# Another distribution of expert dots over a hybrid decoder step's stages, and whole dots that read x from PSUM

## The chip, the cores and the metric

One core of a Trainium2 chip runs the whole program. The metric is the device time of one execution in microseconds; lower is better. PE is the matrix engine, VectorE (DVE) and ScalarE (ACT) compute on tiles, GpSimd (POOL) here issues the indirect DMAs, SyncE (SP) the plain ones.

## What is computed

One layer of a decoder in float32, for a prompt of 1024 tokens and for eight sequences of four new tokens (32 rows, "the sample") that attend to 1024 cached tokens each. Cut to what matters here:

```python
xn = rms_norm(x, attn_norm_w); q_lat, c_kv, k_pe, rq, rk, rv, rg = split(xn @ w_in)
h = x + concat([attention(q, k, v), silu(rg) * group_norm(retention(rq, rk, rv))]) @ w_o
# the PEER feed-forward, on xb = rms_norm(h, ffn_norm_w)
q = (xb @ w_peer_q).reshape(n, 8, 2, 128)
s1, s2 = q[:, :, 0] @ sub_keys1.T, q[:, :, 1] @ sub_keys2.T     # 8 heads, 128 keys each
v1, i1 = top_k(s1, 16); v2, i2 = top_k(s2, 16)
vs, ic = top_k(v1[..., :, None] + v2[..., None, :], 16)          # 16 experts of 16384 per head
act = gelu(einsum('nd,nhkd->nhk', xb, peer_u[experts]))          # the dots
y = h + einsum('nhk,nhkd->nd', softmax(vs) * act, peer_v[experts])
```

Each of the 1024 tokens picks 8 x 16 = 128 experts, and each expert is one row of 4 KB in `peer_u` and one in `peer_v`.

## The kernel before

The prompt is worked in eight tiles of 128 tokens; the sample is a ninth tile, numbered 8, of 32 tokens, whose attention is threaded into tiles 1, 2 and 3. Tokens lie on the 128 partitions. A **slot** is the work on the k-th expert of every token of a tile: 128 slots a tile, and for the sample 32 (its 32 tokens are spread over 128 partitions). A slot has two halves. First the **u row**: POOL gathers 128 rows of `peer_u` into one of 8 buffers (`u_ring`, `u_rows`, L799), and VectorE multiplies it with x and sums, the **dot** (`dot`, L1776), in two instructions of 512 columns, each followed by an accumulator read, with a partial sum each in `dots_2` and `dots`. For each group of 32 slots VectorE adds the partial sums, ACT applies gelu (L1346), VectorE the gates and a transpose, and ACT writes the coefficients into the matrix Z (`make_Z`). Then the **v row**: POOL gathers 128 rows of `peer_v` into one of 9 buffers (`v_rows`, L816), and PE adds them, weighted by Z, into two PSUM banks (`v_row`, L856), 33 slots behind the dots (`V_LAG`). POOL issues v and u rows in turn; a u row waits for the dot that frees its buffer, a v row for PE.

All else of the tile, its **front**, is written out by hand on each engine in the same order of stages: PROJECT (ten weight pieces; in tiles 2, 4 and 6, the hosts, also those of the next tile, their guest), QKV (heads, norms, retention), ATTEND (ten steps, one head each with a shift between scores, probability transposes and the product with v), in tile 1 the sample's mixer, in tiles 2 and 3 a batch of cached pages of four sequences, OUT (output projection, norm), PEER (nine steps; step s holds PE's queries of head s and VectorE's selections of head s - 1). Heads 6 and 7 of a tile are selected during the next tile's PROJECT.

What sets the order is a **pace**. Between the pieces of the front every engine calls `slots()` at the same numbered places, the **sites**. Tables of numbers (`FRONTS`, `PEER`, `LAST`, L543 to L557) say by how many slots the work advances at each site; `sites()` (L559) sums them into bounds, and at a site VectorE computes the dots up to its bound, PE the v rows up to the bound less 33, ACT what falls due of gelu, Z and results. The slots run one tile behind: the front of tile t carries slots of tile t - 1 until step `TURN_OVER` = 4 of its PEER stage, and the first of its own behind. So a front of tiles 1 to 7 carries 95 slots outside PEER and 33 in it, and tile 0's PEER stage 18.

PSUM has eight banks. Banks 0 and 1 hold the v rows' sum; `bank(i)` is bank 2 + i. The keys' scores of the PEER stage lie in banks 6 and 7, the transposed probabilities of a head in bank 4 and, for tiles 4 to 7, also 5, the product with v in bank 6.

## Time and profile before

| what | value |
|---|---|
| median of 3 runs | 3480.07 us (3473.72 to 3485.91) |
| the profiled execution | 3479.65 us |
| its span in the profile | 3477.9 us |
| granted clock of PE, mean | 0.803 |
| busy: PE, DVE, ACT, POOL | 71%, 71%, 12%, 61% |
| moved by DMA | 1321.87 MB, 380 GB/s on average |
| of it the indirect queue | 1107.43 MB |

How to read it: the page gives each engine's busy time; the forty slices of the span carry, under each other, tenths of busy time, PE's clock, the DMA engines' share and GB/s. A query on windows gives the same for chosen stretches. Groups list instructions by source line and shape, with busy time, mean duration and what ended the idle time before them. Groups on DVE under L1751 and L1755 are helpers that issue most of VectorE's instructions.

### The profile page before, as it was taken

How to read it: one execution, taken by the hardware profiler on the slowest of the kernel's cores; microseconds unless marked ns; L12 is line 12 of the kernel's file. 1: busy time of each engine (PE TensorE's matmuls, PEld its weight loads, DVE VectorE, ACT ScalarE, POOL GpSimd, SP SyncE). 2: the span in 40 equal slices, each digit the busy share in tenths (PEclk: the TensorE clock that was granted, in tenths of full speed). 3: DMA queues.
4: the chain of work that ended last, by engine and by line, in shares of the span. 5: the costliest groups of instructions: out<-in, count | busy, mean ns of one | idle time of the engine just before them, and what ended most of it. 6: DMA issues, size and time to landing. Idle time of an engine off the chain costs nothing.

```text
span 3477.9 us, 37700 instructions
## 1 busy us (share of the span) xinstructions
PE 2486.0 (71%) x11828; PEld 1260.8 (36%) x11828; DVE 2468.6 (71%) x8388; ACT 432.7 (12%) x980; POOL 2135.6 (61%) x2118
## 2 busy tenths in 40 slices
PE   6768656888756687696666777697766776678567
PEld 5644124644432334362331234363331233324200
DVE  4587757768678886767578766777578766948652
ACT  1101000113101221111001110111101110000000
POOL 0136755566646665647756775647756775677876
PEclk8879677898877888898886778898887788775667
DMA  6479999999999999999999999999999999999999
GB/s 256 170 266 393 383 347 388 389 382 357 392 399 367 391 370 391 411 370 410 410 410 406 410 409 407 397 368 410 411 410 400 410 406 408 381 411 383 348 409 369
DMA packets 373386, 1321.87 MB, mean 380 GB/s; under 512 B 60962, under 2 KB 72418, under 8 KB 352962
## 3 DMA queue, kind: packets, MB, share of 16 engines
q0 software_dynamic: 304128, 1107.43, 81.2%
q1 hardware_dynamic: 69058, 212.03, 15.7%
q8 instruction: 93, 1.52, 0.2%
q14 instruction: 107, 0.88, 0.1%
HBM read 1311.41 MB, written 7.88 MB: 379 GB/s over the span
## 4 chain that ended last, share of the span: by engine, by line
PE 26%; DVE 23%; DMA 22%; POOL 17%; issue 9%; SPq 2%; ACT 1%; DVEq 0%; ACTq 0%
DMA u_ring<-up_rows,codes 10%; POOL v_ring L824 9%; POOL u_ring L811 8%; DMA v_ring<-down_rows,codesT 8%; PE ps L932 7%; DVE u_ring L1785 7%; PE ps L869 6%; DMA wbuf<-weights 4%; DVE arena L1751 3%; PE ps L922 3%; PE ps L1132 2%; PE ps L1185 2%; DVE idx L1751 1%; DVE top_c L1751 1%; DVE top_v L1751 1%
## 5 line engine op out<-in xcount | busy, mean ns | idle before, releaser
L1785 DVE CUSTOM_DVE_ANT_0 u_ring<-u_ring,xn 128x512 f32<-128x512 f32 x2112 | 1345.7, 686 | 510.7 <-DMA u_ring<-up_rows,codes 506.3
L811 POOL DMA_INDIRECT u_ring<-up_rows,codes x1056 | 1077.4, 1020 | 769.6 <-issue 291.8
L869 PE MATMUL ps<-v_ring,Z 128*32 128x512 f32 x4096 | 1082.6, 757 | 613.8 <-DMA v_ring<-down_rows,codesT 474.6
L824 POOL DMA_INDIRECT v_ring<-down_rows,codesT x1056 | 1057.0, 1001 | 559.0 <-issue 284.4
L869 PEld LDWEIGHTS ps<-v_ring,Z 128*32 128x32 f32 x4096 | 147.9, 121 | 1222.2 <-DMA v_ring<-down_rows,codesT 918.0
L1132 PEld LDWEIGHTS ps<-xT,wbuf 128*128 128x128 f32 x2176 | 312.0, 229 | 200.0 <-issue 119.1
L1132 PE MATMUL ps<-xT,wbuf 128*128 128x128 f32 (+1 forms) x2176 | 337.4, 318 | 57.1 <-DMA wbuf<-weights 57.1
L932 PE MATMUL ps<-wbuf,xT 128*128 128x256 f32 (+2 forms) x1184 | 285.4, 399 | 64.9 <-DMA wbuf<-weights 34.8
L932 PEld LDWEIGHTS ps<-wbuf,xT 128*128 128x128 f32 (+1 forms) x1184 | 226.4, 198 | 141.4 <-DMA wbuf<-weights 47.8
L1785 DVE DVE_READ_ACCUMULATOR2_ANT dots<- 128x1 f32 x2112 | 170.4, 81 | 0.0
L1751 DVE MAX8 vals<-arena 128x8 f32<-128x128 f32 (+1 forms) x288 | 68.8, 279 | 79.1 <-ACT arena L1565 78.4
L1088 PE MATMUL ps<-kT,qT 96*128 96x512 f32 (+3 forms) x192 | 103.0, 656 | 23.7 <-DVE nb L1755 19.4
L922 PE MATMUL ps<-wbuf,kT 128*128 128x256 f32 (+1 forms) x480 | 104.7, 371 | 0.0
L1527 ACT ACTIVATE arena<-arena,nb 128x128 f32<-128x128 f32 (+7 forms) x64 | 49.6, 775 | 354.7 <-DVE nb L1755 354.7
L922 PEld LDWEIGHTS ps<-wbuf,kT 128*128 128x128 f32 x480 | 88.9, 190 | 11.1
L1106 PEld LDWEIGHTS ps<-vN,arena 128*128 128x128 f32 x576 | 78.0, 211 | 8.5 <-issue 7.4
L1106 PE MATMUL ps<-vN,arena 128*128 128x64 f32 x576 | 80.1, 289 | 0.0
L1088 PEld LDWEIGHTS ps<-kT,qT 96*128 96x128 f32 x192 | 39.8, 239 | 111.2 <-issue 74.6
L1751 DVE FIND_INDEX8 idx<-vals,arena 128x8 uint32<-128x128 f32 (+1 forms) x288 | 78.1, 282 | 0.0
L1565 ACT ACTIVATE arena<-ps 128x256 f32<-128x256 f32 (+1 forms) x72 | 27.4, 380 | 371.6 <-PE ps L1142 329.7
L1557 ACT ACTIVATE arena<-ps 128x256 f32<-128x256 f32 (+1 forms) x72 | 26.3, 365 | 353.3 <-PE ps L1132 353.3
L1755 DVE TENSOR_REDUCE arena<-arena 128x8 f32<-128x512 f32 (+1 forms) x72 | 49.2, 683 | 27.4 <-ACT arena L1665 24.5
(337 smaller groups left out, 2425.2 us busy)
## 6 DMA issues: line engine op xcount, KB each, us to landing
wbuf<-weights SPq DMA_DIRECT2D x142, 1024.0 KB, 8.2
u_ring<-up_rows,codes POOLq DMA_INDIRECT x1056, 12.3
v_ring<-down_rows,codesT POOLq DMA_INDIRECT x1056, 12.2
u_ring<-weights SPq DMA_DIRECT2D x8, 1024.0 KB, 13.5
v_ring<-weights SPq DMA_DIRECT2D x8, 1024.0 KB, 13.8
wbuf<-weights SPq DMA_DIRECT2D x9, 768.0 KB, 7.7
resid<-x_prompt SPq DMA_DIRECT2D x8, 512.0 KB
table<-decay_in SPq DMA_DIRECT2D x8, 512.0 KB
```

Of the source, the lines that this page charges most:

```text
L811: pool.indirect_dma_start(out=u_ring[:, i % U_RING, :], out_offset=None, in_=up_rows, in_offset=bass.IndirectOffsetOnAxis(ap=codes[:, t % ...
L824: pool.indirect_dma_start(out=v_ring[:, v % V_RING, :], out_offset=None, in_=down_rows, in_offset=bass.IndirectOffsetOnAxis(ap=codesT[:, t ...
L869: mm = pe.matmul(acc[q:q + 32, half, :], (Zs if t == TILES else Z)[:, at:at + GS], v_ring[:, v % V_RING, half * 512:(half + 1) * 512], sta ...
L922: mm = pe.matmul(ps[:, 2 + S_BANK[w // 2], (w % 2) * PIECE:(w % 2) * PIECE + cols], xT_of(t + 1)[:, c], weights_of(t, w)[:, c, 0:cols], st ...
L932: mm = pe.matmul(out, xT[:, c, 0:n], weights_of(t, w)[:, c, 0:cols], start=(c == 0), stop=(c == DC - 1))
L1088: mm = pe.matmul(ps[:, 2 + c // 512, 0:e - c], qT[0:QK, s, :], kT[0:QK, s, c:e], start=True, stop=True)
L1106: mm = pe.matmul(ps[:, 6, h * 64:(h + 1) * 64], probT[:, h % 2, j * P:(j + 1) * P], vN[:, j, h * 64:(h + 1) * 64], start=(j == 0), stop=(j ...
L1132: mm = pe.matmul(ps[:, 4 + s % 2, j * P:j * P + n], weights_of(t, w)[:, c, j * P:(j + 1) * P], xT[:, c, 0:n], start=(c == 0), stop=(c == D ...
L1185: pe.matmul(ps[0:n, 6 + m % 2, :], lhs, uk, start=True, stop=True).then_inc(kn_ps, 1)
L1527: own.raises(act.activation(scores[:, s % 2, 0:w], scores[:, s % 2, 0:w], ACT.Exp, bias=nb[:, s:s + 1], scale=SCALE, accum_out=sums[:, s:s ...
L1751: own.done(instruction_of(*args, **kwargs))
L1785: ins = dve.tensor_tensor_reduce(u, u, xn[:, t % 2, of], 1.0, 0.0, ALU.mult, ALU.add, into)
```

## The change

The tables get other numbers. Slots of the front by stage, summed from the tables (before, after):

| tile | PROJECT | QKV | ATTEND | mixer or batch | OUT | PEER |
|---|---|---|---|---|---|---|
| 0 | 0, 0 | 0, 0 | 0, 0 | | 0, 0 | 18, 32 |
| 1 | 23, 26 | 12, 12 | 12, 10 | 37, 21 | 11, 8 | 33, 33 |
| 2 | 22, 33 | 12, 9 | 12, 10 | 37, 32 | 11, 11 | 33, 33 |
| 3 | 19, 25 | 12, 12 | 14, 11 | 40, 36 | 11, 11 | 33, 33 |
| 4 and 6 | 23, 34 | 15, 16 | 40, 27 | | 17, 18 | 33, 33 |
| 5 and 7 | 18, 26 | 18, 20 | 43, 31 | | 16, 18 | 33, 33 |
| sample | | | | | 32, 32 | 52, 52 |

The last site carries 58 slots before and 62 after. `TURN_OVER` is 5: a tile's own slots begin one step later in PEER, but in tile 0, which has a table of its own, two steps earlier. Tile 0 selects all eight heads in its own PEER stage.

In ATTEND from its third site, OUT and PEER (tiles 1 to 3: from the end of the mixer or batch) ACT copies x into banks 6 and 7, once for the slots of the tile before and once for the tile's own, and a dot is then one instruction of 1024 columns whose x comes from PSUM. These are 512 of the 1024 prompt slots; the first three own slots of a tile stay halves. The sample's 32 dots read x from the banks in which PE spreads it, and ACT's two copies of it go. To free banks 6 and 7, key scores move to banks 2 and 3, the product with v to bank 5, and the transposed probabilities of tiles 4 to 7 share bank 4: PE turns four blocks, then multiplies, then waits for VectorE's copy of the four and turns the rest, which ACT copies. PE waits for the last copied key scores before the next tile's first transposes, and for the last whole dot before piece 4 of PROJECT. Only halved dots are still summed in pairs.

```diff
+        x_now = ps[:, 6:8, :]
+        x_spread = ps[:, 2:4, :]
...
-        PROJECT = [3, 3, 4, 4, 3, 3]
-        QKV = [3, 2, 3, 3, 2, 2]
-        ATTEND = [4] * H + [5, 5]
+        PROJECT = [4, 4, 4, 5, 4, 4]
+        QKV = [2] * 6
+        ATTEND = [4] * H + [4, 4]
...
-            FRONTS[t] = [3, 3, 4, 4, 4, 5] + QKV + [4] * H + [4, 4] + [4, 3, 4, 2, 2, 2]
+            FRONTS[t] = [4, 5, 5, 5, 8, 7] + [2, 3, 3, 2, 4, 2] + [3] * 7 + [2, 2, 2] + [5, 3, 3, 2, 3, 2]
...
+        FIRST_PEER = [[0, 0], [0, 0], [0, 2], [3, 3], [3, 3], [3, 3], [2, 3], [2, 3], [1, 1]]
-        TURN_OVER = 4
+        TURN_OVER = 5
...
             def project_all(t, n, slots):
+                if t:
+                    pe.wait_ge(keys_copied, H * t)
                 turn(t, 0, mix, n)
...
                     if t and w == 4:
-                        pe.wait_ge(keys_copied, H * t)
+                        pe.wait_ge(dot_done, X_RANGES[t - 1][1])
...
-                    for j in range(t + 1):
-                        mm = pe.transpose(ps[:, 4 + j // 4, (j % 4) * P:(j % 4 + 1) * P],
-                                          scores[:, (s - 1) % 2, j * P:(j + 1) * P], ident[:])
+                    for j in range(min(t + 1, 4)):
+                        mm = pe.transpose(ps[:, 4, j * P:(j + 1) * P], scores[:, (s - 1) % 2, j * P:(j + 1) * P], ident[:])
                     mm.then_inc(probT_ps, 1)
...
+                if 1 <= s <= H and t >= 4:
+                    pe.wait_ge(probT_a, H * (t - 4) + s)
+                    for j in range(4, t + 1):
+                        mm = pe.transpose(ps[:, 4, (j - 4) * P:(j - 3) * P], scores[:, (s - 1) % 2, j * P:(j + 1) * P], ident[:])
+                    mm.then_inc(probT2_ps, 1)
...
+            def load_x(t, of_own):
+
+                if of_own:
+                    act.wait_ge(dot_done, t * SLOTS)
+                    act.wait_ge(wide_ready, wide_no(t, 2))
...
+                own.raises(act.activation(x_now, src, ACT.Copy), x_loaded, 2 * t - 1 + of_own)
...
+                load = x_load_of(i)
+                if load:
+                    dve.wait_ge(x_loaded, load)
...
+                if load or t == TILES:
+                    u = u_ring[:, i % U_RING, :].rearrange("p (a b) -> p a b", a=2)
+                    ins = dve.tensor_tensor_reduce(u, u, x_spread if t == TILES else x_now, 1.0, 0.0, ALU.mult, ALU.add, dots[:, k:k + 1])
+                else:
...
             HEADS_HERE = 6
+            WHOLE = (0, TILES - 1, TILES)
...
-                here = HEADS_HERE if t + 1 < TILES else H
+                here = H if t in WHOLE else HEADS_HERE
```

How the built program moves. VectorE in tile 0's PEER stage, behind the codes of head 1 (`codes`, their transpose `codesT`); `MAX vals` opens a head's selection and `ISA u_ring,dots` is half a dot. Before:

```order
L2057 SCALAR_TENSOR_TENSOR codes<-e 128x16
L1755 STREAM_TRANSPOSE codesT<-codes 128x32
L1751 MAX vals<-arena 128x8 x2
L1751 MAX_INDEX idx<-vals,arena 128x8 x2
L1751 MATCH_REPLACE arena<-vals,arena 128x128 x2
```

and of the change:

```order
L2143 SCALAR_TENSOR_TENSOR codes<-e 128x16
L1828 STREAM_TRANSPOSE codesT<-codes 128x32
L1865 ISA u_ring,dots<-u_ring,xn 128x512
L1865 ISA dots 128x1
L1865 ISA u_ring,dots<-u_ring,xn 128x512
```

The first dots now stand right behind head 1, where head 2 came before.

PE in ATTEND of tile 4, one step: scores (`kT,qT`), transposes of the head before (`ident,arena`), product with v (`vN,arena`), v rows (`v_ring,Z`, two instructions a row). Before:

```order
L1088 MATMUL ps<-kT,qT 128x512
L1088 MATMUL ps<-kT,qT 128x128
L1097 MATMUL ps<-ident,arena 128x128 x5
L1106 MATMUL ps<-vN,arena 128x64 x5
L869 MATMUL ps<-v_ring,Z 32x512 x8
```

and of the change:

```order
L1134 MATMUL ps<-kT,qT 128x512
L1134 MATMUL ps<-kT,qT 128x128
L1143 MATMUL ps<-ident,arena 128x128 x4
L1151 MATMUL ps<-vN,arena 128x64 x5
L1157 MATMUL ps<-ident,arena 128x128
L912 MATMUL ps<-v_ring,Z 32x512 x6
```

The fifth transpose moves behind the product with v and stands behind a wait; three v rows follow instead of four.

VectorE in OUT of tile 1, behind the mixer, of the change alone: whole dots (`u_ring,ps`) around the two additions to `resid`, where pairs of halves stood before.

```order
L1860 ISA u_ring,dots<-u_ring,ps 128x1024
L1860 ISA dots 128x1
L1824 TENSOR_TENSOR resid<-resid,ps 128x512
L1860 ISA u_ring,dots<-u_ring,ps 128x1024
L1860 ISA dots 128x1
```

Here a dot has one instruction and one accumulator read.

## Rows read from the trace of the kernel before

**Rows 1.** The page: GB/s in the forty slices of the span, and the sum.
```profile
GB/s 256 170 266 393 383 347 388 389 382 357 392 399 367 391 370 391 411 370 410 410 410 406 410 409 407 397 368 410 411 410 400 410 406 408 381 411 383 348 409 369
DMA packets 373386, 1321.87 MB, mean 380 GB/s; under 512 B 60962, under 2 KB 72418, under 8 KB 352962
```

**Rows 2.** Windows: length, busy PE, PEld, DVE, ACT, POOL, then PEclk, DMA share, GB/s.
```profile
139.00:207.90 68.90, 23.57 (x177) 22.36 (x175) 66.08 (x272) 6.93 (x18) 24.78 (x25) 0.68 0.66 225
207.90:257.30 49.40, 46.27 (x211) 31.41 (x211) 36.90 (x144) 4.49 (x12) 18.78 (x20) 0.96 0.93 337
353.00:476.40 123.40, 73.40 (x292) 16.51 (x292) 95.44 (x270) 5.97 (x20) 87.62 (x79) 0.65 0.94 359
634.10:764.40 130.30, 112.48 (x579) 78.89 (x579) 87.08 (x297) 19.09 (x40) 71.03 (x72) 0.92 0.99 382
796.10:909.50 113.40, 94.05 (x507) 46.17 (x511) 95.02 (x258) 35.99 (x74) 70.41 (x73) 0.82 0.95 357
1195.90:1316.40 120.50, 96.47 (x525) 45.94 (x526) 99.28 (x272) 35.74 (x73) 77.25 (x79) 0.84 0.95 355
1461.20:1598.30 137.10, 119.08 (x599) 78.88 (x599) 92.16 (x311) 19.10 (x40) 77.15 (x78) 0.91 0.99 385
2242.70:2378.00 135.30, 116.17 (x599) 76.97 (x601) 92.68 (x311) 18.97 (x40) 77.38 (x79) 0.94 0.99 383
2747.40:2860.40 113.00, 82.39 (x401) 36.42 (x400) 79.73 (x233) 19.71 (x34) 82.11 (x83) 0.88 1.03 407
3114.70:3280.50 165.80, 122.63 (x482) 60.03 (x482) 125.90 (x489) 8.47 (x27) 127.25 (x97) 0.57 0.97 373
```

**Rows 3.** Timeline of POOL, then VectorE, sample PEER stage: start us, us, instruction.
```profile
3184.77 4.54 POOL L811 DMA_INDIRECT u_ring<-up_rows,codes  x1 [0.30 <-issue]
...
3184.76 0.67 DVE L1785 CUSTOM_DVE_ANT_0 u_ring<-u_ring,xn 128x512 f32<-128x512 f32 x1
3185.37 0.68 DVE L1785 CUSTOM_DVE_ANT_0 u_ring<-u_ring,xn 128x512 f32<-128x512 f32 x1
...
3188.44 0.07 DVE L1785 DVE_READ_ACCUMULATOR2_ANT dots<- 128x1 f32 x1
```

**Rows 4.** Timeline of POOL, then VectorE, attention of tile 7.
```profile
2795.68 0.94 POOL L824 DMA_INDIRECT v_ring<-down_rows,codesT  x1 [0.30 <-issue]
2796.92 0.94 POOL L811 DMA_INDIRECT u_ring<-up_rows,codes  x1 [0.31 <-issue]
...
2795.70 0.70 DVE L1785 CUSTOM_DVE_ANT_0 u_ring<-u_ring,xn 128x512 f32<-128x512 f32 x1
2796.33 1.21 DVE L1988 CUSTOM_DVE_ANT_0 arena<-ps,table 128x1024 f32<-128x1024 f32 x1
2797.48 0.08 DVE L1988 DVE_READ_ACCUMULATOR2_ANT mx<- 128x1 f32 x1
```

**Rows 5.** Groups of VectorE, then PE, 2747 to 2860 us (attention of tile 7).
```profile
L1988 DVE CUSTOM_DVE_ANT_0 arena<-ps,table 128x1024 f32<-128x1024 f32 x8 | 9.8, 1221 | 4.5 <-PE ps L1088 3.9 <-issue 0.6
L1755 DVE COPY arena<-ps 128x512 f32<-128x512 f32 x8 | 5.5, 690 | 0.9
...
L869 PE MATMUL ps<-v_ring,Z 128*32 128x512 f32 x172 | 39.7, 683 | 27.6 <-DMA v_ring<-down_rows,codesT 23.4 <-ACT Z L1366 4.2
L1106 PE MATMUL ps<-vN,arena 128*128 128x64 f32 x128 | 15.3, 273 | 0.0
```

**Rows 6.** Timeline of VectorE: first head, second head, first dot of tile 0.
```profile
130.97 0.49 DVE L1751 MAX8 vals<-arena 128x8 f32<-128x128 f32 x2 [8.11 <-ACT arena L1565]
...
139.02 0.49 DVE L1751 MAX8 vals<-arena 128x8 f32<-128x128 f32 x2
...
160.91 0.69 DVE L1785 CUSTOM_DVE_ANT_0 u_ring<-u_ring,xn 128x512 f32<-128x512 f32 x1
```

**Rows 7.** Groups of POOL, 3114.7 to 3280.5 us (sample PEER stage).
```profile
L811 POOL DMA_INDIRECT u_ring<-up_rows,codes x49 | 69.1, 1411 | 24.2 <-issue 14.0 <-DVE dots L1785 10.2
L824 POOL DMA_INDIRECT v_ring<-down_rows,codesT x48 | 59.1, 1231 | 14.6 <-issue 12.8 <-PE ps L869 1.8
```

More of the change, by code:

```diff
@@ L563, in sites @@
                 at = (t - 1) * SLOTS + sum(sum(two) for two in PEER[TURN_OVER:])
-                if t < TILES:
+                if t == 0:
+                    at, sizes, before, after = 0, [0] * len(FRONTS[0]), sum(FIRST_PEER, []), []
+                elif t == 1:
+                    at = sum(sum(two) for two in FIRST_PEER)
+                if t == 0:
+                    pass
+                elif t < TILES:
                     sizes = FRONTS[t]
@@ L573, in sites, with x_ranges, x_load_of, halved @@
             return bounds
+        def x_ranges():
+            ends, at = [], 0
+            bounds = sites()
+            peer_sites = 2 * (H + 1)
+            for t in range(TILES):
+                first = at + len(PROJECT + QKV) + (2 if t not in (S_TILE,) + B_TILES else len(FRONTS[t]) - len(PROJECT + QKV) - len(OUT) + 1)
+                at += len(FRONTS[t]) + peer_sites
+                ends.append((bounds[first - 1], bounds[at - 1]))
+            return ends
+        X_RANGES = x_ranges()
+        def x_load_of(i):
+            for t in range(1, TILES):
+                begin, end = X_RANGES[t]
+                if begin <= i < t * SLOTS:
+                    return 2 * t - 1
+                if t * SLOTS + 3 <= i < (end if t < TILES - 1 else TILES * SLOTS):
+                    return 2 * t
+            return 0
+        def halved(group):
+            split = [group < GROUPS * TILES and not x_load_of(group * GS + j) for j in range(GS)]
+            begins = [j for j in range(GS) if split[j] and not (j and split[j - 1])]
+            ends = [j + 1 for j in range(GS) if split[j] and not (j + 1 < GS and split[j + 1])]
+            return list(zip(begins, ends))
+        def sums_upto(group):
+            return sum(len(halved(g)) > 0 for g in range(group + 1))
         class Pace:
@@ L1346, in gelu @@
             def gelu(t, g):
-                act.wait_ge(dots_summed, group_no(t, g) + 1)
+                act.wait_ge(dot_done, t * SLOTS + (g + 1) * GS)
+                if halved(group_no(t, g)):
+                    act.wait_ge(dots_summed, sums_upto(group_no(t, g)))
                 at = slice(g * GS, (g + 1) * GS)
@@ L1375, in put_y @@
                 own.raises(act.activation(ybuf, acc.rearrange("p a b -> p (a b)"), ACT.Copy), y_ready, t + 1)
+            def load_x(t, of_own):
+                if of_own:
+                    act.wait_ge(dot_done, t * SLOTS)
+                    act.wait_ge(wide_ready, wide_no(t, 2))
+                elif t == S_TILE:
+                    act.wait_ge(s_R_ready, 4)
+                elif t in B_TILES:
+                    act.wait_ge(s_pT_b, B_TILES.index(t) + 1)
+                else:
+                    act.wait_ge(kT_ready, t + 1)
+                own.wait()
+                src = xn[:, (t if of_own else t - 1) % 2].rearrange("p (a b) -> p a b", a=2)
+                own.raises(act.activation(x_now, src, ACT.Copy), x_loaded, 2 * t - 1 + of_own)
             def groups(done, upto):
@@ L1383, in groups @@
                         gelu(*divmod(at // GS - 1, GROUPS))
+                    if at % SLOTS == 0 and at < SLOTS * TILES:
+                        load_x(at // SLOTS, 1)
                     if at % SLOTS == V_LAG and at > SLOTS:
@@ L1530, in attention @@
                     h = s - 1
-                    act.wait_ge(probT_ps, H * t + h + 1)
+                    if t < 4:
+                        act.wait_ge(probT_ps, H * t + h + 1)
+                    else:
+                        act.wait_ge(probT2_ps, H * (t - 4) + h + 1)
                     if h >= 2:
@@ L1538, in attention @@
                     else:
-                        ins = act.activation(probT[:, h % 2, 512:(t + 1) * P], bank(3, P, (t - 3) * P), ACT.Copy)
+                        ins = act.activation(probT[:, h % 2, 512:(t + 1) * P], bank(2, P, (t - 3) * P), ACT.Copy)
                     own.raises(ins, probT_b, H * t + h + 1)
@@ L1564, in copy_keys @@
                         act.wait_ge(keys_used, H * t + h - 1)
-                    own.raises(act.activation(sS[0:n, h % 2], ps[0:n, 6 + h % 2, 0:256].rearrange("p (j k) -> p j k", j=2), ACT.Copy),
+                    own.raises(act.activation(sS[0:n, h % 2], ps[0:n, 2 + h % 2, 0:256].rearrange("p (j k) -> p j k", j=2), ACT.Copy),
                                keys_copied, H * t + h + 1)
@@ L1611, in project @@
                         lat_squares(t, n)
-                    if w == 5 and t:
+                    if w == 5 and t >= 2:
                         gate_exps(t - 1, P)
@@ L1634, in prompt_front @@
                 slots()
+                if t and t != S_TILE and t not in B_TILES:
+                    load_x(t, 0)
                 for s in range(H + 2):
@@ L1724, in sample_rest @@
                 gate_exps(t, n)
-                act.wait_ge(sample_spread_ps, 1)
-                own.wait()
-                own.done(act.activation(xn[:, 0, 0:512], bank(0), ACT.Copy))
-                own.raises(act.activation(xn[:, 0, 512:1024], bank(1), ACT.Copy), xn_spread, 1)
                 slots()
@@ L2001, in attention @@
                     do(dve.reciprocal, sums[:], sums[:])
-                    do_signal(wide_ready, wide_no(t, 1), dve.tensor_tensor, heads(mix[:, 0:512]), heads(bank(4)),
+                    do_signal(wide_ready, wide_no(t, 1), dve.tensor_tensor, heads(mix[:, 0:512]), heads(bank(3)),
                               over(sums[:], 2, [P, H, 64]), ALU.mult)
```

60 lines of the change are left out of this document (35 added, 25 removed).

## The prediction

> **What bounds the kernel now.** I read the page first. VectorE and PE are each busy 71% of the span (table above), while the GB/s line of the forty slices sits at 406 to 411 wherever nothing disturbs it [rows 1]. So the plateau is about 410 GB/s, and the kernel moves 1321.87 MB: at the plateau that takes 3224 us of the 3478. The other 254 us are time in which the queues had too little to move, and only they can be won. This is the view to learn from: a busy engine is no bound here, a hole in the GB/s is.
>
> Then I cut the span by stages, since a mean hides the holes. Each slot's dot leaves two accumulator reads on VectorE, so counting them gives the time at which any site of the tables was passed; the windows of [rows 2] begin and end at stage borders found that way. For each I take lost time = length x (1 - GB/s / 410). That gives 31.1 and 8.8 us for the two stretches behind the first expert numbers (from 139 us to dot 32 at 257.3), 15.4 for the sample's mixer, 8.9 for tile 2's projection and QKV, 14.7 and 16.2 for the two batches of pages, 8.4 and 8.9 for projection and QKV of tiles 4 and 6, 15.0 for the sample's own PEER stage. The attention of tile 7 loses 0.8: there the plateau holds. In tiles 4 and 6's projection PE is busy 87% and 86% while the dots are few (38 in either); in the batches PE is busy 80 to 83%; behind 139 us VectorE is busy 96%.
>
> What one slot costs: two rows of 0.524 MB, 2.56 us at the plateau. On VectorE a dot of two halves takes 1.23 us when it waits for nothing (halves start 0.61 us apart [rows 3]). On PE a v row takes 39.7 / 43 = 0.92 us [rows 5]. One head's two selections take 139.02 - 130.97 = 8.05 us on VectorE [rows 6].
>
> **The change, part by part.**
>
> *Start of tile 0.* Before, the first dot comes at 160.91 [rows 6], behind nearly four heads; now two dots follow head 1 and 32 instead of 18 lie in this stage, together with heads 6 and 7, which leave tile 1's projection. VectorE is then never idle: 8 x 8.05 + 32 x 1.23 + about 7 us for the two norms and the gates from 130.97 gives dot 32 at 242, against 257.3. By then 49 rows (40 u, 9 v) and some 6 MB of weights and inputs have moved, 31.4 MB or 77 us; 103 - 77 = 26 us are lost, against 39.9. That is 14 us won, not the 36 that 14 dots times 2.56 suggest, because PE's projection of tile 1 (46 busy us by 257.3 [rows 2]) has not begun. It must still run; with 38 slots over PROJECT and QKV, where 35 lay before, I take what is lost behind dot 32 as unchanged. Term: -14.
>
> *Mixer of the sample, tile 1.* From 37 dots to 21. VectorE's own work is 95.4 - 37 x 1.23 = 50 us; with 21 dots 76, and 10 or more of its 28 idle us are waits for PE and ACT that stay. The transfers shrink from 44.3 to 27.5 MB, 67 us. So 19 us are lost instead of 15.4. Term: +4. Bounds 0 and +20 (all 28 idle us stay, 104 - 67 = 37 lost).
>
> *Projection and QKV of tiles 2, 4, 6.* 34 dots become 42, 38 become 50. Tile 4: PE's own work is 119.1 - 38 x 0.92 = 84 us, with 50 dots 130; the transfers grow from 52.8 to 65.4 MB, 159 us. PE no longer ends last. Terms -8.9, -8.4, -8.9: -26. The dots come out of attention (40 to 27) and the batches.
>
> *Batches of tiles 2 and 3.* 37 to 32 and 40 to 36 dots. Between the two batches three dots make 7.1 us [rows 2], 2.4 us a dot, nearly the 2.56 of its transfers: each dot taken away frees as much time as traffic. Lower bound of that price is PE's 0.92, where 9 dots cost 9 x 1.64 = 15 us. I take the measured 2.4: +2.
>
> *Attention of tiles 4 to 7.* The probability transposes now share one bank: PE turns four blocks, multiplies head s-2, waits for VectorE's copy (0.69 us), then turns the rest. Behind that wait on PE stand the rest, the v rows of the site and the next head's scores, for which VectorE waits. In tile 7 PE's own work for a head is about (82.4 - 39.7) / 8 = 5.3 us, with 3.1 v rows 8.2; the transfers for 3.1 slots and the mask take 8.2. VectorE needs 1.22 + 0.69 [rows 5], up to 2.9 of group norm, 3.1 dots 3.8: 6 to 9 us. PE's multiply with v (15.3 / 8 = 1.9 us) and first transposes cover reduction and copy if VectorE is in time. So the cover of this part is about gone in tiles 6 and 7; in tiles 4 and 5, with five and six of the eight blocks, PE's own work shrinks to some 3.3 and 4.0 us (estimated from the 5.3 by blocks) and over 1 us a head is spare. Term: +6; lower bound 0; upper bound in the rivals.
>
> *Whole dots.* 512 of the 1024 prompt slots read x from banks 6 and 7 in one instruction, the sample's 32 from banks 2 and 3. The nearest row is the masked row maximum, same custom operation, 1024 wide, PSUM and SBUF: 1221 ns [rows 5], its accumulator read 1.15 us behind its start [rows 4]. So a whole dot is 0.08 us cheaper, 44 us of VectorE in all, nearly all hidden under the transfers; 14 copies of x go to ACT, which is busy 12% of the span. What counts is POOL. In the sample's PEER stage its calls average 1411 and 1231 ns, not 0.94 [rows 7]: the call at 3184.77 takes 4.54 us, exactly over six halves back to back [rows 3]. A call over the maximum with its PSUM operand takes 0.94 [rows 4]. With calls of 0.94 + 0.30 the stage's 97 need 121 us, and VectorE 126 - 4, both under the 151 us of its bytes. Term: -12 of the 15.0; bounds 0 and -15.
>
> The Trainium skill (GPSIMD Engine Reference, Specifications) says that GpSimd shares its SBUF interfaces with VectorE and contends with instructions that have two SBUF inputs. The long calls agree, but by that rule alone all halves would stretch calls, and in tile 7's attention POOL calls under halves stay at 0.94; by the rule this part is -12, without it 0.
>
> The skill's VectorE: DVE Perf Modes (The TRN2 errata) gives 58 + N cycles from SBUF and 120 + N from PSUM. By that an estimate makes two halves and a whole dot 1.19 us each, and the 44 us of VectorE would be 0; the row of the maximum, the nearer measurement, decides for 0.08 us a dot.
>
> *Smaller waits.* PE waits for the last key copy before it turns the next x, and for the last whole dot before piece 4. ACT's copy lies beside VectorE's last slots, for whose end PE waits anyway with the next xT; the dots are done by then. I take nothing for both; if that cover is gone it is 8 times one copy of 256 columns, under 0.69 us each by VectorE's copy of 512 [rows 5], 5 us.
>
> **Sum.** -14 + 4 - 26 + 2 + 6 - 12 = -40 us. The profiled execution took 3479.65 (span 3477.9), 0.4 below the median of 3480.07. 3479.65 - 40 = 3439 (-1.2%).
>
> **Rivals.**
> *More is won (10%).* All holes of the mixer, the batches and the sample's PEER go as well: a further 60 us, 3380. For it: VectorE gets 44 us back. Against: PE and chains between engines, not VectorE, hold the batches.
> *Given back (22%).* The holes only move: 16 dots fewer in the mixer and 9 in the batches cost their upper bounds (20 and 15) and POOL's calls stay long: -14 + 20 - 26 + 15 + 6 = +1, up to -20; centre 3468. For it: a stage limited by its own chain loses 2.56 us of traffic with each slot taken from it. Against: 2.4 us a dot between the batches.
> *Slower: the new wait in attention (8%).* If VectorE's dots (3.1 x 1.23 = 3.8 us) stand ahead of the copy while PE is idle, each of 32 heads pays 3.8 less what it has to spare (1 us in 16 of them): 106 us, 3479.65 - 46 + 106 = 3540. It decides from 1.5 us a head on (46 / 32). For it: both engines now wait for each other within a head. Against: PE has 3 us of its own work before it needs the copy.
> *The whole dots or the tables do not do what they say:* the built order shows both, so no chance is set aside.
>
> **Numbers.** A measurement here tells about 0.3% (10 us) from no change. Forecast (3415 to 3462) 60%; more 10%; given back 22%, half of it under 3469; slower 8%. Faster 0.60 + 0.10 + 0.11 = 0.81; same 0.11; slower 0.08. The range leaves out the slower rival and half of the rival with more: 3390 to 3474.
>
> **What would show it.** GB/s of 405 or more in the projection and QKV of tiles 4 and 6, with PE under 85%; first dot near 150 us and dot 32 near 242; POOL calls near 0.94 us in the sample's PEER stage; whole dots near 1220 ns; attention of tile 7 at 400 GB/s or more. Wrong if the attention of tiles 6 and 7 falls under 390 GB/s, with PE waiting for VectorE's copy, or if the mixer loses over 30 us.

## The result, and the profile after

The changed kernel takes 3487.03 us (median of 20 runs, 3482.91 to 3499.92), the kernel before in the same comparison 3473.39 (20 runs): ratio 1.0036, 95% interval 1.0024 to 1.0048. Slower by a third of a per cent, where 1.2% faster was forecast. The profiled execution of after took 3492.32 us, its span is 3490.5.

The page of after: GB/s of the forty slices, bytes, and VectorE's two kinds of dots.

```profile
GB/s 255 182 247 368 382 277 379 353 412 364 334 410 376 410 343 380 411 412 411 410 411 396 410 400 411 403 409 408 410 411 375 410 397 408 383 412 411 400 410 361
DMA packets 373382, 1321.83 MB, mean 379 GB/s; under 512 B 60962, under 2 KB 72418, under 8 KB 352962
...
L1860 DVE CUSTOM_DVE_ANT_0 u_ring<-u_ring,ps 128x1024 f32<-128x1024 f32 x544 | 649.4, 1217 | 353.4 <-DMA u_ring<-up_rows,codes 352.6
L1865 DVE CUSTOM_DVE_ANT_0 u_ring<-u_ring,xn 128x512 f32<-128x512 f32 x1024 | 651.8, 687 | 188.3 <-DMA u_ring<-up_rows,codes 185.0
```

The plateau is still 410 to 412 and the bytes are the same, so the holes have moved, not gone. Against [rows 1] the sixth slice (436 to 524 us) fell from 347 to 277, while the right half gained. The windows of after, cut at the same sites as [rows 2] (columns: length; busy PE, PEld, DVE, ACT, POOL; PEclk, DMA share, GB/s):

```profile
139.00:241.00 102.00, 30.21 (x188) 25.84 (x187) 98.74 (x399) 6.07 (x15) 47.01 (x47) 0.64 0.76 276
241.00:329.40 88.40, 71.94 (x360) 44.00 (x361) 43.12 (x140) 9.35 (x24) 40.14 (x41) 0.89 0.91 335
411.70:501.30 89.60, 55.33 (x228) 15.90 (x228) 74.87 (x204) 5.46 (x12) 47.98 (x43) 0.59 0.81 295
541.90:658.40 116.50, 67.77 (x428) 46.47 (x428) 87.25 (x296) 11.77 (x30) 56.32 (x60) 0.76 0.97 366
658.40:799.40 141.00, 120.67 (x609) 80.16 (x611) 97.75 (x330) 19.13 (x40) 90.48 (x90) 0.91 1.03 411
830.60:938.10 107.50, 89.75 (x475) 43.14 (x476) 88.20 (x234) 34.68 (x69) 59.90 (x60) 0.80 0.87 317
1227.80:1343.60 115.80, 92.08 (x503) 44.87 (x503) 94.49 (x256) 37.19 (x75) 69.15 (x70) 0.82 0.90 336
1486.40:1648.60 162.20, 135.44 (x645) 81.51 (x645) 108.18 (x359) 17.84 (x39) 102.16 (x105) 0.89 1.03 411
2261.90:2424.30 162.40, 135.87 (x645) 82.78 (x645) 108.17 (x359) 17.84 (x39) 102.91 (x104) 0.88 1.02 408
2555.10:2662.80 107.70, 74.80 (x404) 43.75 (x404) 85.22 (x281) 12.35 (x32) 58.12 (x62) 0.79 0.98 383
2791.00:2872.20 81.20, 64.06 (x356) 33.10 (x352) 61.26 (x134) 19.14 (x32) 54.23 (x58) 0.87 1.01 396
3131.90:3285.50 153.60, 112.71 (x479) 56.20 (x478) 121.08 (x383) 7.17 (x26) 98.12 (x104) 0.62 1.03 411
```

In order: tile 0's PEER, tile 1's PROJECT, mixer and PEER, tile 2's PROJECT and QKV, the two batches, PROJECT and QKV of tiles 4 and 6, tile 6's PEER, attention of tile 7, the sample's PEER. With lost time = length x (1 - GB/s / 410), as in the prediction, and with the stages between them, the stages up to the last dot add up like this (us lost, two profiled executions; the last 47 us of each lose 8.6 and 10.3 more):

| where | before | after | change | forecast |
|---|---|---|---|---|
| tile 0, to its last slot in PEER | 105.3 | 107.7 | +2 | -14 with the next row |
| tile 1, PROJECT and QKV | 12.4 | 18.9 | +7 | |
| tile 1, ATTEND, mixer, OUT, PEER | 25.5 | 51.9 | +26 | +4 |
| tiles 2, 4, 6, PROJECT and QKV | 26.1 | -0.4 | -26 | -26 |
| batches of tiles 2 and 3 | 30.8 | 45.1 | +14 | +2 |
| ATTEND of tiles 4 to 7 | 1.8 | 5.3 | +4 | +6 |
| PEER of tiles 2 to 7 | 19.3 | 23.2 | +4 | 0 |
| the sample's PEER | 15.1 | -0.2 | -15 | -12 |
| all stages | 245.2 | 256.2 | +11 | -40 |

The rest is 3 us less in the projections of tiles 5 and 7 and 1 in other stages. The large gains came as forecast; tile 1 and the batches took more than all of them. A second pair of traces, the kernel before once more (3481.01 us) and the changed one (3487.89 us), gives +9 and +24 for the two rows of tile 1, -24 for the projections, +10 for the batches and -17 for the sample's PEER: a row is good to about 4 us.

What happens in tile 1 stands in PE's timeline (start, us, instruction, idle time before it and its releaser). Before, with VectorE's copy of tile 1's turned input:

```profile
207.80 0.68 DVE L1755 TENSOR_TENSOR xT<-ps,attn_wc 128x512 f32<-128x512 f32 x1
...
208.53 5.16 PE L932 MATMUL ps<-wbuf,xT 128*128 128x256 f32 x16 [21.36 <-DVE xT L1755]
```

and after, with the rows of VectorE and ACT around it:

```profile
210.73 1.79 PE L896 MATMUL ps<-h_cur,place_p 128*64 128x512 f32 x4
249.79 3.57 PE L912 MATMUL ps<-v_ring,Z 128*32 128x512 f32 x12 [37.27 <-ACT Z L1419]
253.29 3.72 PE L975 MATMUL ps<-wbuf,xT 128*128 128x256 f32 x16
...
239.42 0.17 DVE L2143 SCALAR_TENSOR_TENSOR codes<-e 128x16 uint32<-128x16 f32 x1
245.62 0.69 DVE L1828 TENSOR_TENSOR xT<-ps,attn_wc 128x512 f32<-128x512 f32 x1 [0.25 <-DVEq L77]
248.43 0.21 DVE L1828 STREAM_TRANSPOSE coefT<-gelus 128x32 f32<-128x32 f32 x1
...
248.68 1.06 ACT L1419 ACTIVATE Z<-coefT 32x32 f32<-32x32 f32 x4 [2.85 <-DVE coefT L1828]
```

PE has turned tile 1's input at 208 us and then stands for 37.3 us: VectorE copies the turned input (xT) only at 245.6, behind heads 6 and 7 and the gates, and the first site of tile 1 now carries 4 slots, so three v rows, which need Z, stand ahead of PROJECT's first piece. Before, VectorE copied first and selected heads 6 and 7 beside PE's pieces; PE began at 208.5. All of PE's projection now lies behind the start, 45 us later (253.29 against 208.53), for a dot 32 that is 16 us earlier.

### The profile page after: what moved, and what is told of

It is laid out like the page before. It is cut to its first block, busy times and chain, and to the rows that moved or that the text cites. A ratio compares the mean times of both kernels' runs of the same rounds, so it can differ in the third digit from the quotient of the medians.

```text
span 3490.5 us, 37161 instructions
## 1 busy us (share of the span) xinstructions
PE 2478.7 (71%) x11828; PEld 1267.0 (36%) x11828; DVE 2422.8 (69%) x7298; ACT 446.5 (13%) x990; POOL 2060.5 (59%) x2118
## 4 chain that ended last, share of the span: by engine, by line
DMA 33%; PE 22%; DVE 17%; POOL 10%; issue 8%; SPq 2%; ACT 1%; DVEq 0%; ACTq 0%
DMA u_ring<-up_rows,codes 17%; DMA v_ring<-down_rows,codesT 12%; PE ps L912 6%; POOL v_ring L867 5%; POOL u_ring L854 5%; PE ps L975 4%; DMA wbuf<-weights 4%; DVE u_ring L1865 3%; DVE arena L1824 2%; DVE u_ring L1860 2%; PE ps L1235 2%; PE ps L1182 2%; PE ps L965 2%; DVE arena L1828 1%; DVE idx L1824 1%
## 5 line engine op out<-in xcount | busy, mean ns | idle before, releaser
L912 PE MATMUL ps<-v_ring,Z 128*32 128x512 f32 x4096 | 1061.4, 759 | 650.6 <-DMA v_ring<-down_rows,codesT 454.6
L854 POOL DMA_INDIRECT u_ring<-up_rows,codes x1056 | 1026.0, 972 | 763.7 <-issue 256.8
L867 POOL DMA_INDIRECT v_ring<-down_rows,codesT x1056 | 1033.3, 978 | 653.7 <-PE ps L912 380.2
L1860 DVE CUSTOM_DVE_ANT_0 u_ring<-u_ring,ps 128x1024 f32<-128x1024 f32 x544 | 649.4, 1217 | 353.4 <-DMA u_ring<-up_rows,codes 352.6
L1865 DVE CUSTOM_DVE_ANT_0 u_ring<-u_ring,xn 128x512 f32<-128x512 f32 x1024 | 651.8, 687 | 188.3 <-DMA u_ring<-up_rows,codes 185.0
L1824 DVE MAX8 vals<-arena 128x8 f32<-128x128 f32 (+1 forms) x288 | 68.9, 280 | 89.8 <-ACT arena L1638 89.6
L1134 PE MATMUL ps<-kT,qT 96*128 96x512 f32 (+3 forms) x192 | 91.8, 593 | 18.2 <-DVE nb L1828 14.8
L1865 DVE DVE_READ_ACCUMULATOR2_ANT dots<- 128x1 f32 x1024 | 82.5, 81 | 0.0
```

What stands on the lines that cost most here:

```text
L854: pool.indirect_dma_start(out=u_ring[:, i % U_RING, :], out_offset=None, in_=up_rows, in_offset=bass.IndirectOffsetOnAxis(ap=codes[:, t % ...
L867: pool.indirect_dma_start(out=v_ring[:, v % V_RING, :], out_offset=None, in_=down_rows, in_offset=bass.IndirectOffsetOnAxis(ap=codesT[:, t ...
L912: mm = pe.matmul(acc[q:q + 32, half, :], (Zs if t == TILES else Z)[:, at:at + GS], v_ring[:, v % V_RING, half * 512:(half + 1) * 512], sta ...
L1134: mm = pe.matmul(ps[:, 2 + c // 512, 0:e - c], qT[0:QK, s, :], kT[0:QK, s, c:e], start=True, stop=True)
L1824: own.done(instruction_of(*args, **kwargs))
L1860: ins = dve.tensor_tensor_reduce(u, u, x_spread if t == TILES else x_now, 1.0, 0.0, ALU.mult, ALU.add, dots[:, k:k + 1])
```

## Experiments

The runs were made in five sets, each on one chip with the kernel before beside it; the ratio is to that. In two sets the kernel before took 3476 and 3477 us, as in the main comparison (below: the sets at 3476), in three it took 3707 to 3750 (the sets at 3740). That is a difference of the surroundings, and it turns a sign (last section), so runs are compared within a kind of set. "Chip" in the expectations means this.

**The start as before.** Tile 0 has 18 slots in its PEER and leaves heads 6 and 7 to tile 1's PROJECT.

```diff
-        FRONTS[1] = [4, 4, 5, 5, 4, 4] + [2] * 6 + [1] * (H + 2) + [2, 2, 3, 2, 2, 2, 2, 2, 2, 2] + [2, 1, 2, 1, 1, 1]
+        FRONTS[1] = [3, 3, 4, 4, 4, 5] + [2] * 6 + [1] * H + [2, 2] + [4, 3, 4, 3, 3, 4, 4, 4, 3, 3] + [1, 2, 1, 2, 1, 2]
-        FIRST_PEER = [[0, 0], [0, 0], [0, 2], [3, 3], [3, 3], [3, 3], [2, 3], [2, 3], [1, 1]]
+        FIRST_PEER = [[0, 0]] * 4 + PEER[4:]
...
-            WHOLE = (0, TILES - 1, TILES)
+            WHOLE = (TILES - 1, TILES)
```

> The changed kernel with tile 0 and the front of tile 1 as before: 18 dots in tile 0's PEER, heads 6 and 7 of tile 0 in tile 1's PROJECT, 91 slots in tile 1's front (35 in the mixer). All else as changed. Theory A (the change loses its gain in tile 1, whose front loses 71 us against 38 before, while the start is no better, 108 against 105): the 33 us come back but for about 4, so about 3458 us, and PE's one wait of 37.3 us for the first Z is gone. Theory B (the whole dots with x from PSUM, or the new waits of PE that protect their banks, make every stage slower): tile 1 keeps most of its 33 us, 3480 or more.

Measured 0.9834 (0.9792 to 0.9875), in a set at 3740 and without the changed kernel beside it, so it decided nothing. Again in a set at 3476:

> The changed kernel with tile 0 and tile 1's front as before (the run of the first set again, on this chip). Of the change's loss, tile 1 holds 33 us (lost 71 against 38) on chips where the kernel before takes 3475. If all that comes from what the change does up to the end of tile 1's front: 25 to 30 us under the changed kernel, 3460, 0.4% under the kernel before. If tile 1 loses it anyway, since whole dots and the waits for their banks delay PE in its mixer: 3480 or more.

Measured 3460.62 us, 0.9954 (0.9938 to 0.9969), against 1.0040 (1.0027 to 1.0053) for the changed kernel in the other set at 3476: 30 us, give or take 7. The PROJECT and the mixer of tile 1 in this kernel:

```profile
207.90:279.50 71.60, 69.44 (x314) 44.10 (x315) 54.21 (x197) 6.82 (x19) 31.88 (x32) 0.97 0.96 361
356.90:474.30 117.40, 69.56 (x266) 16.95 (x268) 92.81 (x258) 7.65 (x25) 77.43 (x71) 0.59 0.90 346
```

PE is busy 97% of PROJECT, in after 81%, and the stage is 17 us shorter (3 slots fewer in it). So what the change does up to the end of tile 1's front costs some 30 us, and without it the change is a gain of 0.5%.

**An early copy.** All eight heads stay in tile 0, but the turned input is copied before heads 6 and 7, and no v row stands ahead of PE's first four pieces.

```diff
-        FRONTS[1] = [4, 4, 5, 5, 4, 4] + [2] * 6 + [1] * (H + 2) + [2, 2, 3, 2, 2, 2, 2, 2, 2, 2] + [2, 1, 2, 1, 1, 1]
+        FRONTS[1] = [1, 0, 3, 6, 7, 9] + [2] * 6 + [1] * (H + 2) + [2, 2, 3, 2, 2, 2, 2, 2, 2, 2] + [2, 1, 2, 1, 1, 1]
...
+                    if t + 1 == S_TILE and s == HEADS_HERE + 1:
+                        first_copies(t + 1, P)
                     if 1 <= s <= here:
                         peer(t, s - 1, n, slots)
```

(`first_copies` holds VectorE's copies of tile 1's and the sample's turned input, taken out of `project`; ACT's is moved likewise.)

> The changed kernel, where VectorE and ACT copy tile 1's transposed input as soon as PE has it (before heads 6 and 7 of tile 0 are selected, not behind all eight and the gates), and tile 1's first three PROJECT sites carry 1, 0 and 3 slots, so that no v row, and with it no wait for the first Z, stands ahead of PE's first four pieces. Theory A1 (of the 33 us, the serial start of the projection is the larger part): PE computes from about 213 us instead of 250, the project stage ends some 25 to 30 us earlier with the same dots, the time is 3460 to 3467. Theory A2 (the loss is that the mixer, OUT and PEER of tile 1 now have too few slots for their own chain of work, 25, 10 and 12 us lost): these three stay as they are and only the 16 us of PROJECT can come back, 3471 or more; if what is won is lost again behind it, 3487.

Measured 0.9815 (0.9773 to 0.9857), in the set at 3740 that had no control; tile 1's QKV, with its 70th dot, ended at 374.5 us there, and at 388.4 and 394.6 in two others of the set. It is repeated below, on the tables alone.

**Tables alone, and with the early copy.** The kernel before with the change's tables, `TURN_OVER` and place of heads, and nothing of its dots, banks and waits; then the same with the early copy and its first sites; beside them the changed kernel and the kernel before.

> The changed kernel as the control of this chip. On two chips so far, where the kernel before takes 3707 to 3738 us and not 3473, the change was ahead by 1.2%; where this chip stands is what the run tells: with the kernel before near 3475 it should be 0.4% behind, with the kernel before near 3710 1.2% ahead.

> The kernel before with the tables of the change, its TURN_OVER and all eight heads of tile 0 in tile 0, but halves everywhere, the old banks and none of PE's new waits: the complement of the run that had the new dots and banks alone. There these cost 0.7% of the kernel before (1.0039 to 1.0096) and the whole change gained 1.2%. If the parts add up: 1.9% under the kernel before on such a chip, 0.7% under the changed kernel; on a chip like the first 3465. If the tables gain only together with whole dots (VectorE free for the longer bursts in PROJECT, POOL in the sample's PEER): no better than the changed kernel, with 15 us or more lost in the sample's PEER stage.

> The kernel with the tables alone, and tile 1's transposed input copied before heads 6 and 7 of tile 0, with 1, 0 and 3 slots in tile 1's first PROJECT sites, as in the earlier run with the early copy. There tile 1's PROJECT and QKV ended at 374.5 us against 384 to 395 in the others with 58 and 70 dots at the same places. So 10 to 16 us under the kernel with the tables alone, and the fastest of the four. If what is won there is lost again in the mixer, OUT and PEER of tile 1, no difference.

Measured in this set at 3476: the changed kernel 3488.03 us, 1.0040 (1.0027 to 1.0053), the first result again; tables alone 3500.45, 1.0069 (1.0056 to 1.0082); with the early copy 3490.01, 1.0039 (1.0027 to 1.0052). The tables cost 24 us and the rest of the change gains 12. The first expectation for the tables, which added up parts from a set at 3740, was wrong. The early copy, with its first sites, wins 10.4 us. PE with it:

```profile
217.65 6.45 PE L939 MATMUL ps<-wbuf,xT 128*128 128x256 f32 x16 [13.89 <-DVE xT L1765]
...
236.07 5.38 PE L939 MATMUL ps<-wbuf,xT 128*128 128x256 f32 x16 [3.74 <-DMA wbuf<-weights]
...
251.20 6.73 PE L939 MATMUL ps<-wbuf,xT 128*128 128x256 f32 x16 [6.19 <-DMA wbuf<-weights]
...
263.50 1.91 PE L876 MATMUL ps<-v_ring,Z 128*32 128x512 f32 x12
```

With the tables alone PE began its first piece at 249.88, so the early copy brings it 32 us sooner, yet only 12 us of that arrive at the end of QKV (370.2 against 381.7): the pieces wait for their weights, and the first v rows come behind four pieces. So the late projection explains about a third of the 30 us, as far as 10 us measured on the tables alone hold for the changed kernel.

**More slots in the mixer.** If the mixer loses because it has too few slots, slots from PROJECT should help it.

```diff
-        FRONTS[1] = [4, 4, 5, 5, 4, 4] + [2] * 6 + [1] * (H + 2) + [2, 2, 3, 2, 2, 2, 2, 2, 2, 2] + [2, 1, 2, 1, 1, 1]
+        FRONTS[1] = [2, 2, 3, 3, 2, 2] + [2] * 6 + [1] * (H + 2) + [4, 3, 3, 4, 3, 3, 4, 3, 3, 3] + [2, 1, 2, 1, 1, 1]
```

> The changed kernel with 33 slots in the mixer of tile 1 instead of 21, and 14 in PROJECT instead of 26. The mixer took 89.6 us with 21 slots and 123.4 with 37 (kernel before): 2.1 us a slot, against 2.56 of transfers. Theory M (the mixer's loss of 25 us comes from too few slots for its own chain of work): 12 more slots make it 115 us and take its loss to about 19, PROJECT shortens by 12 times 0.92 to 77 us or by more; tile 1's front ends 3 to 10 us earlier or not at all later. Theory S (what costs tile 1 its time is the serial start of PE's projection, which then has even less to cover it): PROJECT's loss grows from 16 to 30 us and the time is that of the changed kernel or up to 10 us more.

Measured 3500.99 us, 1.0067 (1.0051 to 1.0083): 13 us slower than the changed kernel by the medians of the two sets at 3476, 9 by the ratios. Theory M is out; theory S has the direction, though PROJECT's loss grew to 20 us and not to 30. The changed kernel was not in this set. Its PROJECT, QKV and mixer:

```profile
240.20:306.10 65.90, 57.19 (x276) 36.35 (x277) 27.44 (x90) 8.76 (x23) 20.81 (x21) 0.91 0.82 283
306.10:364.00 57.90, 44.37 (x254) 25.38 (x252) 31.38 (x93) 7.64 (x15) 29.50 (x30) 0.85 0.86 320
398.20:510.60 112.40, 72.21 (x276) 17.90 (x276) 89.92 (x249) 5.47 (x12) 74.57 (x65) 0.61 0.89 328
```

PROJECT and QKV lose 20.4 and 12.7 us, together 33 against 19. The mixer takes 112.4 us with 33 slots, 89.6 with 21: 1.9 us a slot, under the 2.56 of its transfers. So each slot taken from it should lose 0.7 us, but by the windows the 33 slots lost 22.5 us there against 25.2, only 0.2 a slot. Each slot put back cost more where PE's late projection needs cover. Tile 1 has 18 slots fewer in its front, 14 of them spent at the start. That it is that many short wherever they are put fits this run, but no run gives it more slots and keeps the start.

**Dots, banks and waits alone.** The changed kernel with every table as before.

> The changed kernel with every table, TURN_OVER and the place of heads 6 and 7 of tile 0 as before: what is left of the change is the whole dots, the moved banks and the waits of PE. Theory A (the loss of the change lies in its tables for tiles 1 to 3): the 15 us of the sample's PEER come back and little else changes, 15 us under the kernel before, 0.996. Theory B (the bank layout costs time: attention with one bank for the transposes, the waits before the next tile's transposes): no gain or a loss, 1.000 or more, with attention of tiles 4 to 7 under 400 GB/s.

> The new dots, banks and waits with every table as before (the run of the second set again). There it was 0.7% slower than the kernel before. On a chip where the kernel before takes 3475, tables alone cost 24 us and the whole change 12 to 14, so whole dots should give 12: 3464, 0.9965, nearly all in the sample's PEER stage (17 us lost, then none). If the whole dots pay only with the new tables: no faster than the kernel before, with losses in the attention of tiles 4 to 7, which has 40 and 43 slots here.

In the set at 3740 it was slower, 1.0067 (1.0039 to 1.0096); in one at 3476 3460.27 us, 0.9953 (0.9937 to 0.9969), 16 us gained. Attention of tile 7 and the sample's PEER in the latter, and PE's waits for VectorE's copy in that attention (total, times, longest):

```profile
2750.40:2863.50 113.10, 82.35 (x398) 37.41 (x396) 76.82 (x164) 20.64 (x34) 80.04 (x85) 0.81 1.03 409
3116.40:3274.30 157.90, 118.26 (x476) 57.32 (x476) 121.33 (x383) 8.45 (x27) 97.89 (x105) 0.61 1.03 410
...
PE ps L1157 <- DVE arena L1828: 14.3, 6, 4.6
```

The new wait is there, 14.3 us, and costs nothing: the stage has 409 GB/s with 43 slots. In this set the shared bank is free.

**Halves.** Two runs ask where whole dots count.

```diff
         def x_load_of(i):
 
+            return 0
```

> The changed kernel with every prompt dot again in two halves with x from SBUF (ACT's copies of x into banks 6 and 7 and PE's waits stay; the sample's 32 dots stay whole). If whole dots matter only by VectorE's 0.08 us each, hidden under the transfers: 3487, no change. If they free POOL, whose calls then issue earlier in attention and PEER: 3490 to 3500. Theory B (x from PSUM costs time, by the bank or by POOL): 3475 or less.

> The changed kernel with prompt dots whole only where they are tile 7's own (79 of the 512), all others in halves. Theory P (the use of whole dots is that POOL's calls are no longer held up in the sample's PEER stage, where 52 slots follow each other closely; elsewhere they are hidden): the same time as the changed kernel within 5 us. Theory Q (VectorE's 0.08 us a dot and POOL count in every stage): 15 us or more behind the changed kernel.

> The changed kernel itself, as the control on the same chip as the three others. Every theory: 0.4% behind the kernel before (1.0024 to 1.0048), as first measured, if the chip moves bytes as the first one did.

Both fell in sets at 3740. All prompt dots in halves: 0.9866 (0.9828 to 0.9904), with 34.0 us lost in the sample's PEER where the other three of its set lost 6.0 to 10.5; the total shows no clear difference and there was no control. In the other set of that kind, this stage lost 3.2 us in the changed kernel, 12.1 with only tile 7's own dots whole and 18.6 with whole dots and the old tables, so the figure varies much at 3740. Whole for tile 7's own slots alone: 0.9864 (0.9828 to 0.9900), the changed kernel beside it 0.9876 (0.9840 to 0.9911): no difference, theory P. POOL in the sample's PEER, after and then with tables alone (halves):

```profile
L854 POOL DMA_INDIRECT u_ring<-up_rows,codes x52 | 49.3, 948 | 36.5 <-DVE dots L1860 25.0 <-issue 11.6
L867 POOL DMA_INDIRECT v_ring<-down_rows,codesT x52 | 49.1, 944 | 19.1 <-issue 11.6 <-PE ps L912 7.5
```

```profile
L818 POOL DMA_INDIRECT u_ring<-up_rows,codes x48 | 68.6, 1429 | 20.4 <-issue 13.7 <-DVE dots L1792 6.7
L831 POOL DMA_INDIRECT v_ring<-down_rows,codesT x48 | 60.5, 1260 | 14.6 <-issue 11.9 <-PE ps L876 2.7
```

A call has 0.95 us beside whole dots with x in PSUM, 1.43 and 1.26 beside halves, as in [rows 7]; 14 us are lost there with halves, none with whole dots. The rule of the Trainium skill that the prediction weighed (GPSIMD Engine Reference, Specifications: interfaces shared, contention with two SBUF inputs) agrees with this stage.

**The batches.** Tables of tiles 2 and 3 as before, on the changed kernel; then tile 3's alone on the kernel with the old start.

> The changed kernel with the tables of tiles 2 and 3 as before (37 and 40 slots in the batches, 34 and 31 in PROJECT and QKV). If a slot in a batch is worth what the loss there says (24.3 and 20.8 us lost now, 14.6 and 16.2 before), the batches give back 14 us and tile 2's projection takes 9: about 3482, no more than 0.2% from the changed kernel. If the batch's own work were so well covered that each slot moved out saves its 2.4 us, as the prediction took it, the batches give back 2 and the projection takes 9: 3494.

> As the kernel with tile 0 and tile 1's front as before, and tile 3's table as before too (40 slots in its batch instead of 36, 31 in PROJECT and QKV instead of 37). Tile 3's PROJECT and QKV lose nothing at either number, its batch 16.2 with 40 and 20.8 with 36: 4 to 5 us under the kernel it is made from. Tile 2 stays as changed, since there PROJECT gives back as much as the batch takes. If the slots are worth their transfers wherever they stand: no difference.

The first, in a set at 3740: 0.9908 (0.9868 to 0.9948), no control beside it. The second, at 3476: 3457.16 us, 0.9940 (0.9923 to 0.9956), the fastest kernel of the study, 0.6% under the kernel before and, by the two ratios, 1.0% under the changed one. Its lead of 3.5 us over the one with the old start has the forecast size, but the intervals overlap, and its batch of tile 3 still loses 20 us with 40 slots:

```profile
1186.30:1310.90 124.60, 100.12 (x520) 49.63 (x522) 99.26 (x270) 36.99 (x75) 78.94 (x80) 0.81 0.91 343
```

So slots alone do not give that batch back what it had before, and the cause of that stays open. The kernel it is made from has this batch with 36 slots:

```profile
1206.50:1322.20 115.70, 92.18 (x505) 44.88 (x506) 94.31 (x256) 37.25 (x75) 69.54 (x70) 0.82 0.86 316
```

Between these two kernels, which differ in nothing but tile 3's table, a slot is worth (124.6 - 115.7) / 4 = 2.2 us.

**Tiles 4 and 6 alone, tile 2 as before.**

> The kernel before, in which only the table of tiles 4 and 6 is that of the change (50 slots in PROJECT and QKV instead of 38, 27 in ATTEND instead of 40). Theory A (what the stages lost there, 8.5 and 8.8 us, comes back in full since attention has cover): 17 us under the kernel before, ratio 0.995. If attention or the next PEER stage loses it again (the change lost 2.8 and 7.0 us in the PEER stages of tiles 4 and 6): 7 us, 0.998.

> The kernel with the new dots, banks and waits and every table as before, in which tiles 4 and 6 get 50 slots in PROJECT and QKV instead of 38 (3, 4, 4, 4, 9, 10 in PROJECT) and 27 in ATTEND instead of 40. Without them it was 0.47% under the kernel before. Theory H (PROJECT and QKV of tiles 4 and 6 lose 8.1 and 8.9 us there and would lose none): 17 us less, 0.9905, the fastest of all. Theory G (what is won there is lost again in the next PEER stages, 3 and 6 us, and through bursts of 9 and 10 slots): 5 to 8 us less, 0.993 to 0.994.

> The kernel with the start and tiles 1 and 3 as before (0.9940 of the kernel before), and tile 2's table as before too: 34 slots in its PROJECT and QKV instead of 42, 37 in its batch instead of 32. If a slot moved from batch to PROJECT only moves the loss: the same within 5 us, with 9 us lost in PROJECT and QKV and 5 to 9 less in the batch. If the projection's gain was the larger: 4 to 9 us more. If the batch's: 3 to 5 us less.

All three fell in sets at 3740: 0.9928 (0.9896 to 0.9959), 0.9975 (0.9946 to 1.0004) and 0.9884 (0.9853 to 0.9915). In the first, tiles 3 and 5 form their first coefficients with the gates of the tile before: with `TURN_OVER` 4 this table passes slot 418 before the new gates are there. That is what `TURN_OVER` 5 is for, and it holds four slots back in every tile. So the table of tiles 4 and 6 gains 0.7% there with halves. With whole dots the only comparison is across two sets (0.9975 against 1.0067), whose kernels before differ by more than that, 3749.93 and 3706.52, and the medians stand the other way round (3745.07 against 3730.51): nothing is shown. None of the three says anything of the sets at 3476.

## Why the prediction was wrong, point by point

- *What bounds the kernel*, a plateau of 410 GB/s and holes in it: right as an account, since the bytes are the same and the span grew by what more was lost. It says where time goes, not which step opens a hole.
- *Start of tile 0, -14*: the step that failed. Dot 32 came at 241.0 (forecast 242) and the first dot at 148; from 139 us on 33 us were lost (the first window above, GB/s 276) where 26 were forecast, so 6 us were won there and not 14. But the sentence "I take what is lost behind dot 32 as unchanged" had its refutation beside it: 46 busy us of PE that no longer lay under VectorE's selections. Behind dot 32 PROJECT and QKV of tile 1 lost 3.6 us before and 18.9 after. The prediction should have asked what PE does from 208 to 250 us; the built order shows the copy of xT behind heads 6 and 7, and the v rows ahead of the pieces. Measured with all that hangs on it, the rest of tile 1's front too: 30 us lost, not 14 won. Of these the early copy recovers 10. For the rest, that tile 1 has fewer slots to cover its own chain is an argument; the runs show only that the loss is gone with the old start and front, and that moving slots within the front does not win it back.
- *Mixer, +4*: it took 89.6 us, not the 86 (67 of transfers and 19 lost) of the sum, and lost 25. A slot is worth 1.9 us there. ATTEND, OUT and PEER of tile 1, with no term, lost 17 us more (27 against 10); in the kernel with the old start and front they lose 12, so most of it goes with them, but no run takes it apart.
- *Projection and QKV of tiles 2, 4 and 6, -26*: right, -26, at 408 to 411 GB/s, with PE busy 84% in tiles 4 and 6.
- *Batches, +2*: mis-sized, +14. A slot frees (113.4 - 107.5) / 5 = 1.2 us in the first and (120.5 - 115.8) / 4 = 1.2 in the second, near the lower bound of 0.92 that the prediction named, not the 2.4 that it took from the difference of the two batches (7.1 us for three slots). The second pair of traces gives 1.2 in both again. But where tile 3's table alone was changed, a slot was worth 2.2, so no single price holds for these stages, and why is open.
- *Attention, +6*: the size was near (+4), the cause was not. With the bank shared and the old tables nothing is lost; with the new tables and the old banks tile 7 loses 4.4 us.
- *Whole dots, -12*: right, -15, at the forecast place; 12 and 16 us in two comparisons. Two whole dots start 1.14 us apart in the trace, against 1.23 for two halves: 0.09 us saved a dot, 0.08 forecast.
- *Smaller waits, 0*: the price was right, the cover was not what I said. PE does wait for the last key copy before it turns tile 1's input, once for 19.9 us, far over the 0.69 allowed a copy, since that copy stands behind VectorE's selections:

```profile
PE ps L912 <- ACT Z L1419: 37.3, 1, 37.3
PE ps L923 <- ACT arena L1638: 19.9, 1, 19.9
```

  It costs nothing in the changed kernel because PE waits for xT and Z behind it anyway. With the early copy it cost little either: in the changed kernel with that copy PE turned the input at 204.05, behind a wait of 19.9 us, and began its pieces at 215.53; with the tables alone, which lack this wait, it turned it at 199.69 and began at 217.65, when VectorE had made the copy.
- *Not in the sum*: PEER of tile 6 (7 us lost, 5 in the second trace) and of tile 4 (3 in both), which lost nothing before. They follow the larger PROJECT stages; that these are the cause was not tried.
- The rival that came nearest is "given back": its +20 for the mixer and +15 for the batches were near the truth (+26 with its neighbours, +14), but it kept the -14 of the start, added nothing for it, and left out the -12 of the whole dots, which came. Its total of +1 at most falls short of the 14 measured. The rival on the slower side named attention, and there nothing happened.
- *The signs that were named*: nearly all that spoke for the forecast came (411 and 408 GB/s with PE at 84%, dots at 148 and 241, calls of 0.95 us, whole dots of 1217 ns; only tile 7's attention had 396 GB/s and not 400), and neither that spoke against it. None of them looked at tile 1's projection.

Added up, in sets at 3476: whole dots and banks -16, start +30, the other tables 0 (0.9954 against 0.9953). Those other tables win 26 us in the three projections and lose 17 in the batches, by the stages of these two runs, and 9 in PEER.

## What to carry to other kernels

When work is moved ahead of a point, look for what the other engine did beside the work that was there: here PE's projection ran beside two heads on VectorE, and the dots came 16 us earlier while the projection began 45 us later. Price a moved slot by a run that moves it and nothing else: the difference of two stages said 2.4 us, two kernels with other tables around the stage 1.2, one table alone 2.2. And a gain in one stage, a sound one, says nothing until the stages that paid for it are summed too.
